# Second MLP: feature block 6 of the down projection by half-size products, block 7 over two rounds, last parts in another tile order

## The reference, cut to what matters

```python
def rms_norm(x, gain):
    y = x * lax.rsqrt(jnp.mean(x * x, axis=-1, keepdims=True) + EPS)
    return y * gain

def sq_relu_mlp(h, w_up, w_down):
    return jnp.square(jax.nn.relu(h @ w_up)) @ w_down

for i in range(DEPTH):                       # DEPTH = 2
    ...                                      # the mixer: retention, then gated DeltaNet
    ff = sq_relu_mlp(rms_norm(h, gains[2]), mlp_w_up[i], mlp_w_down[i])
    h = h + rms_norm(ff, gains[3])
```

## Time and profile before

| | us |
|---|---|
| three runs | 1400.92, 1404.13, 1404.32; median 1404.13 |
| the profiled execution | 1400.85 |
| its span, first to last instruction | 1399.1 |
| mean granted TensorE clock, share of full speed | 0.998 |
| busy: PE / DVE / ACT / POOL | 1386.6 / 948.6 / 711.4 / 289.4 |

### The profile page before, as it was taken

One profiled execution on the slowest core, in us unless ns is written; L12 is line 12 of the kernel. 1 busy time (PEld: TensorE's weight loads), 2 busy tenths in 40 slices (PEclk: granted clock), 3 DMA queues, 4 the chain that ended last, 5 costly groups with the idle time before them and its releaser, 6 DMA issues.

```text
span 1399.1 us, 19288 instructions
## 1 busy us (share of the span) xinstructions
PE 1386.6 (99%) x7537; PEld 1171.4 (84%) x7538; DVE 948.6 (68%) x1444; ACT 711.4 (51%) x1280; POOL 289.4 (21%) x159
## 2 busy tenths in 40 slices
PE   9999999999999999999999999999999999999998
PEld 7988888658899888888889988889989988888886
DVE  5869779662274877877538534797746777877735
ACT  6235455453364655455345477764835754445442
POOL 6320000443520000000151235357431000000031
PEclk9999999999999999999999999999999999999999
DMA  6522332901325323223432142221115333332131
GB/s 219 208 90 108 146 115 85 350 10 60 98 90 206 121 91 109 82 81 120 142 104 96 47 149 75 87 82 41 61 61 171 105 117 121 120 112 99 61 136 61
DMA packets 69213, 155.27 MB, mean 111 GB/s; under 512 B 4225, under 2 KB 4609, under 8 KB 67458
## 3 DMA queue, kind: packets, MB, share of 16 engines
q1 hardware_dynamic: 66514, 144.78, 30.4%
q10 hardware_dynamic: 2608, 9.25, 1.9%
HBM read 143.52 MB, written 10.50 MB: 110 GB/s over the span
## 4 chain that ended last, share of the span: by engine, by line
PE 94%; DVE 2%; ACT 2%; POOL 1%; issue 1%; DVEq 0%; ACTq 0%; POOLq 0%
PE banks L645 27%; PE banks L647 27%; PE banks L646 27%; PE banks L897 2%; PE banks L880 1%; PE banks L801 1%; PE banks L1070 1%; PE banks L1026 1%; PE banks L701 1%; POOL w_lo L525 1%; PE banks L812 1%; PE banks L915 0%; PE banks L1274 0%; PE banks L1264 0%; PE banks L787 0%
## 5 line engine op out<-in xcount | busy, mean ns | idle before, releaser
L525 POOL TENSOR_TENSOR w_lo<-w_raw,w_hi 128x1024 fp32r<-128x1024 f32 (+1 forms) x86 | 198.4, 2332 | 990.8 <-ACT w_hi L1792 602.9
L645 PE MATMUL banks<-act_hi,w_hi 128*128 128x512 f32 (+1 forms) x800 | 288.7, 361 | 0.5 <-DVE act_lo L2248 0.3
L646 PE MATMUL banks<-act_lo,w_hi 128*128 128x512 f32 (+1 forms) x800 | 287.5, 359 | 0.0
L647 PE MATMUL banks<-act_hi,w_lo 128*128 128x512 f32 (+1 forms) x800 | 287.5, 359 | 0.0
L645 PEld LDWEIGHTS banks<-act_hi,w_hi 128*128 128x128 f32 x800 | 151.1, 189 | 23.6 <-DVE act_lo L2248 0.7
L647 PEld LDWEIGHTS banks<-act_hi,w_lo 128*128 128x128 f32 x800 | 151.1, 189 | 22.6
L646 PEld LDWEIGHTS banks<-act_lo,w_hi 128*128 128x128 f32 x800 | 151.1, 189 | 22.1
L1767 ACT ACTIVATE t_hi<-quarter 128x1024 fp32r<-128x1024 f32 x84 | 88.7, 1056 | 88.1 <-PE banks L647 87.1
L645 PE MATMUL banks<-t_hi,fast_hi 128*128 128x512 f32 x336 | 130.7, 389 | 0.0
L646 PE MATMUL banks<-t_lo,fast_hi 128*128 128x512 f32 x336 | 130.7, 389 | 0.0
L647 PE MATMUL banks<-t_hi,fast_lo 128*128 128x512 f32 x336 | 130.7, 389 | 0.0
(11 more groups left out here) (343 smaller groups left out, 2930.3 us busy)
## 6 DMA issues: line engine op xcount, KB each, us to landing
w_raw<-in_mlp_w_up_dram SPq DMA_DIRECT2D x32, 1024.0 KB, 5.3
quarter<-in_mlp_w_down_dram SPq DMA_DIRECT2D x48, 512.0 KB, 6.4
w_raw<-in_gdn_w_in_dram SPq DMA_DIRECT2D x16, 1024.0 KB, 5.6
w_raw<-in_ret_w_in_dram SPq DMA_DIRECT2D x14, 1024.0 KB, 6.6
vg<-in_ret_w_in_dram SPq DMA_DIRECT2D x8, 1024.0 KB, 10.3
w_raw<-in_ret_w_out_dram SPq DMA_DIRECT2D x8, 1024.0 KB, 5.2
w_raw<-in_mlp_w_down_dram SPq DMA_DIRECT2D x8, 1024.0 KB, 5.0
kept<-resid SPq DMA_DIRECT2D x2, 2048.0 KB, 7.6
```

Of the source, the lines that this page charges most:

```text
L525: done = nc.gpsimd.tensor_tensor(LO[slot][:, kt, :], RAW[raw][:, kt, :], HI[slot][:, kt, :].bitcast(F32), ALU.subtract)
L645: pe.matmul(dst, sta_hi, mov_hi, start=first, stop=False, skip_group_check=adds)
L646: pe.matmul(dst, sta_hi, mov_lo, start=False, stop=False, skip_group_check=adds)
L647: return pe.matmul(dst, sta_lo, mov_hi, start=False, stop=last, skip_group_check=adds)
```

## The change

The second MLP has seven rounds (`FASTS = (6, 7)`); the first one is left as it was. Block 6 is computed by half-size products. The up parts of block 7 are spread over rounds 5 and 6: in round 5 the four of the first half (U0 to U3) come behind P0, P2, P4 and P6, in round 6 the four of the second half (U4 to U7) behind P0 to P3. Only block 7 goes the plain way, in eight *end parts* of 12 matmuls in the order of `END_ORDER`: halves p=0 (now in banks 4 to 7) and p=1 (banks 0 to 3) of a tile soon after each other. The down weights of block 7 are two chunks. ACT's and DVE's lists get a part of their own for round 6 and the end.

```diff
-FAST = 6
+FASTS = (6, 7)
+END_ORDER = ((0, 0), (0, 1), (1, 0), (1, 1), (0, 2), (1, 2), (0, 3), (1, 3))
...
@@ SP: stream_mlp @@
-                for u in range(FAST):
+                for u in range(6):
                     chunk(u + 3, 1)
-                    if u + 1 < FAST:
+                    if u + 1 < fast:
                         quarters(u + 1)
-                    chunk(u + 4, 0)
-                sp.wait_ge(sem("prod_full"), VG_T + 14 * FAST * (layer + 1))
+                    if u + 4 <= PARTS or fast < PARTS - 1:
+                        chunk(u + 4, 0)
+                sp.wait_ge(sem("prod_full"), VG_T + 14 * (done_before + fast))
...
@@ PE: mlp @@
+                def end_part(p, m):
+                    mm = slice(m * P, (m + 1) * P)
+                    for kt in range(CK):
+                        if m == 0:
+                            if kt % (CK // 2) == 0:
+                                pe.wait_ge(w_ready, 2 * (c1 + p) + 1 + kt // (CK // 2))
+                            pe.wait_ge(sem("hid_low"), base + 7 * fast + kt + 1)
+                        done = three(bank[4 * (1 - p) + m][:, :], plain_hi[layer][0][:, kt, mm], plain_lo[layer][0][:, kt, mm],
+                                     HI[p][:, kt, :], LO[p][:, kt, :], kt == 0, kt == CK - 1)
+                    done.then_inc(bank_full, 1)
...
+                if fast == PARTS - 1:
+                    for s in range(7):
+                        product(PARTS - 3, s)
+                        if s in (0, 2, 4, 6):
+                            up_part(PARTS - 1, s // 2)
+                    for s in range(7):
+                        product(PARTS - 2, s)
+                        if s < 4:
+                            up_part(PARTS - 1, 4 + s)
+                    pe.wait_ge(emptied, 4 * g1)
+                    for p, m in END_ORDER:
+                        if (p, m) == (1, 0):
+                            pe.wait_ge(sem("x_out"), 8 * VG + 8 * (done_before + fast))
+                            pe.wait_ge(sem("w_out"), 6 * VG + 6 * (done_before + fast))
+                        end_part(p, m)
+                    return
...
-                if layer:
-                    for m, j in ((0, 0), (1, 0), (0, 1), (1, 1), (2, 0), (2, 1), (3, 0), (3, 1)):
-                        last_part(1, m, j, m == 0)
-                    return
...
@@ ACT: mlp, round 6 @@
+                    take_tile(v, 2)
+                    plain_high(v, 0)
+                    t_high(u, 4)
+                    take_tile(v, 3)
+                    plain_high(v, 1)
+                    t_high(u, 5)
+                    plain_high(v, 2)
+                    split(PARTS, 0)
+                    t_high(u, 6)
+                    plain_high(v, 3)
+                    split(PARTS, 1)
...
@@ DVE: first_half @@
+                if b == 4:
+                    take_out(b, 0, 0, more)
+                    take_out(b, 0, 1, more)
+                    gained(0)
+                    gained(1)
+                    last_tile(0)
+                    last_tile(1)
+                    for m in (2, 3):
+                        take_out(b, 0, m, more)
+                        gained(m)
+                        last_tile(m)
+                    return
...
@@ DVE: mlp, end of round 6 @@
+                    take_product(u, 4)
+                    plain_low(v, 2)
+                    t_low(u, 6)
+                    plain_low(v, 3)
+                    take_product(u, 5)
+                    take_product(u, 6)
+                    dve.wait_ge(sem("resid_back"), 16 * (layer + 2))
+                    first_half(2 * layer + 2, True)
+                    return
```

More of the change, by code:

```diff
@@ L168, in hybrid_trunk @@
                 for b in range(2)] for a in range(2)]
-    plain_hi = [[big(f"plain_hi{a}{b}", [P, 4, T], F32R, PLAIN_AT[a][b][0]) for b in range(2)] for a in range(2)]
-    plain_lo = [[big(f"plain_lo{a}{b}", [P, 4, T], F32R, PLAIN_AT[a][b][1]) for b in range(2)] for a in range(2)]
+    plain_hi = [[big(f"plain_hi{a}{b}", [P, 4, T], F32R, at[0]) for b, at in enumerate(PLAIN_AT[a])] for a in range(2)]
+    plain_lo = [[big(f"plain_lo{a}{b}", [P, 4, T], F32R, at[1]) for b, at in enumerate(PLAIN_AT[a])] for a in range(2)]
     s3_made = big("s3_made", [P, 2, 2 * P], F32, 97)
@@ L553, in low_plain @@
                 c1 = MLP[layer][1][1]
-                for c in range(c1, c1 + 4):
+                for c in range(c1, c1 + 2 * (PARTS - FASTS[layer])):
                     pool.wait_ge(w_ready, 2 * c)
@@ L1750, in plain_high @@
                     act.wait_ge(sem("squared"), tiles + TT * v + m + 1)
-                    act.wait_ge(sem("prod_full"), VG_T + 14 * (FAST * layer + FAST - 1))
-                    act.activation(plain_hi[layer][v - FAST][:, m, :], relu[:, m, :], ACT.Copy)\
+                    act.wait_ge(sem("prod_full"), VG_T + 14 * (done_before + fast - 1))
+                    act.activation(plain_hi[layer][v - fast][:, m, :], relu[:, m, :], ACT.Copy)\
                         .then_inc(sem("hid_high"), 1)
                 def t_high(u, p):
-                    unit = FAST * layer + u
+                    unit = done_before + u
                     q = 7 * unit + p
@@ L1812, in mlp @@
                 take_tile(1, 2)
-                for u in range(FAST):
+                for u in range(fast if fast < PARTS - 1 else fast - 1):
                     w, v = u + 1, u + 2
@@ L2262, in norms @@
             def norms(b, more=False):
-                if b == 4:
-                    for m in range(TT):
-                        last_tile(m)
-                elif b:
+                if b:
                     take_out(b, 1, 0, more)
@@ L2556, in plain_low @@
                 def plain_low(v, m):
-                    dve.wait_ge(sem("hid_high"), base + 7 * FAST + 4 * (v - FAST) + m + 1)
-                    if v == PARTS - 1 and m == 0:
-                        dve.wait_ge(sem("t_ready"), VG_T + 7 * (FAST * layer + FAST - 1) + 4)
-                    dve.tensor_tensor(plain_lo[layer][v - FAST][:, m, :], relu[:, m, :],
-                                      plain_hi[layer][v - FAST][:, m, :].bitcast(F32), ALU.subtract)\
+                    dve.wait_ge(sem("hid_high"), base + 7 * fast + 4 * (v - fast) + m + 1)
+                    if layer == 0 and v == PARTS - 1 and m == 0:
+                        dve.wait_ge(sem("t_ready"), VG_T + 7 * (done_before + fast - 1) + 4)
+                    dve.tensor_tensor(plain_lo[layer][v - fast][:, m, :], relu[:, m, :],
+                                      plain_hi[layer][v - fast][:, m, :].bitcast(F32), ALU.subtract)\
                         .then_inc(sem("hid_low"), 1)
                 def add_up(u, k):
-                    unit = FAST * layer + u
+                    unit = done_before + u
                     q = 7 * unit
```

150 lines of the change are left out of this document (92 added, 58 removed).

## The result

| | before | after |
|---|---|---|
| median of the runs, us | 1404.18 (6 runs, 1400.92 to 1404.32) | 1416.59 (6 runs, 1414.23 to 1417.23) |
| the profiled execution / its span, us | 1400.85 / 1399.1 | 1417.07 / 1415.3 |
| mean granted clock | 0.998 | 0.996 |

The change makes the kernel slower: ratio 1.0092, 95% interval 1.008 to 1.0103. (A ratio compares all runs of both kernels and is not the ratio of the two medians.) The prediction said slower, 1413.5 us in a range of 1405.5 to 1418.

The account below looks back on a forecast made before the run. PE was taken to bound the kernel (busy 99% of the span). -2.72 (matmuls) + 7.8 (waits) + 5.9 (end) = +11.0 us gave 1411.9 on the profiled execution, 1415.1 on the median; middle 1413.5, range 1405.5 to 1418.

Parts of the forecast that it names:

- 12 matmuls fewer: On PE, 96 matmuls of the last parts go and 84 of seven products come: one group fewer, -2.72 us.
- P3 and P4 late: Round 5: DVE's in-order queue delivers the low parts for P3 and P4 late, 1.84 us in all.
- P5 late: Round 6: ACT's `t_hi` for P5 stands behind tile 3's relu, square and split; PE waits 1.75 us.
- P6 late: Round 6: POOL's weight split takes turns with DVE and delays the last `t_lo`; PE waits 4.2 us.
- P6 at half clock: Round 6: PE's clock falls during P6's wait, so P6 takes twice its 2.72 us; left out of the main sum.
- from the last product's end: Last product's end to span's end: late residual load, then DVE's own chain and the last store, 34.6 us.
- against 28.7 before: PE's 21.8 us of end parts plus 6.9 to the span's end; the predicted end is 5.9 us longer.
- the prediction's lower bound: Round 6, P6's wait: 0.7 us if POOL were not in the way of the last `t_lo`.
- The rival without turns: Round 6: POOL and DVE do not alternate, last wait 0.7 to 1.85 us; +7.5 to +8.7; chance 0.20.
- the clock's rival: Round 6: P6's wait lowers PE's clock and P6 takes twice its 2.72 us; +13.7, 1414.6 to 1417.8; chance 0.12.
- The end follows PE: Rounds without waits, DVE ready at each end part: saved group comes through whole, -2.7 us, 1401.4; chance 0.08.
- only the end pays: Rounds 5 and 6 absorb DVE's and ACT's lateness, the 34.6 us end remains: +3.2 us, 1407.3; chance 0.10.

Follow-up runs that it names:

- round 5's experiment: Changed kernel with one up part of round 5 (U2) moved from behind P4 to between P3 and P4: 1415.69 us, ratio 1.0103 to the kernel before.
- the last kernel: Changed kernel with rounds 5 and 6 reordered, residual loaded early, end tile by tile, half-gain and up-weight split moved later: 1400.17 us, ratio 0.9992 to the kernel before.

## Why the prediction was right, step by step

| term | predicted | measured in the profile after |
|---|---|---|
| 12 matmuls fewer | -2.72 | -2.72 (7525 matmul records for 7537) |
| P3 and P4 late | 1.84 | 1.59 (0.41 + 1.18) |
| P5 late | 1.75 | 1.57 |
| P6 late | 4.2 | 3.78 |
| P6 at half clock | 0 (a rival: +2.7) | 1.7 (4.41 - 2.72) |
| from the last product's end | 34.6 | 1415.3 - 1380.06 = 35.2 |
| against 28.7 before | +5.9 | +6.5 |
| sum | +11.0 | +12.4; whole difference +12.8 |

- **PE's waits** came where they were named, and were 0.9 less together. A part of that is the start behind a wait: it was put at 0.25 behind the end of `t_lo`, and PE started 0.09 to 0.10 behind it each time. The edits show the causes as predicted: DVE's order in round 5, ACT's order at P5, POOL's turns with DVE at P6 (and some 0.5 of ACT's order there, the 0.7 of the prediction's lower bound). The rival without turns (a last wait of 0.7 to 1.85) is out: the `t_lo` took 3.37, and without POOL beside it 1.22.
- **What was off is the clock's term.** The prediction set it to nothing and gave it 0.12 as a rival with 2.7 us. In the profile after it cost 1.7, since eight of P6's twelve matmuls ran at the lower level and not all. Filling the wait took 1.6 away.
- **The end** is as worked out: the load lands 8.3 us after its issue (7.9 predicted), DVE's tail takes 24.5 (24.3). The 0.6 on top is the load (0.4) and DVE's tail (0.2). The load's excess is scatter of the runs as far as they show: with the gains' load issued 4.7 us ahead of it in both, it took 8.29 here and 7.75 in round 5's experiment.
- **About 0.4 us** of the 12.8 stands in no term. Some 0.3 of it is seen: P3, P4 and P5, each behind a wait, take 2.83 to 2.84 us instead of 2.72. In each the second matmul starts 0.30 or 0.31 and not 0.23 behind the first.
- **How near, and by what luck.** By the medians the change costs 12.4 us; the forecast of 1413.5 is 9.4 above the median that it started from. The prediction added its sum to two bases, the profiled execution and the median 3.3 above it, and took the middle; the sum on the median, 1415.1, was the better base, and with the clock's 1.7, less 0.9 of waits, plus 0.6 at the end it comes to 1416.5. So the measured 1416.59 lies above both forms of the main sum (1411.9 and 1415.1) and in the band of the clock's rival (1414.6 to 1417.8). The waits and the end were foreseen; that the time lies inside the range is owed to the room left for that rival.
- **Rivals.** "The end follows PE" and "only the end pays" fell with PE's waits. Yet in the last kernel, after six edits, the end does follow PE. The residual early was a condition of it, as the prediction said. The half-gains ahead of the last tiles were not: there DVE still took 5.59 us per tile, and it fell behind PE's 5.44 only when the half-gain went into DVE's wait inside the last tile.

## What to carry to other kernels

A saving on the engine that sets the time shortens the rounds in which the other engines prepare its operands; lay their lists beside the new due times product by product, since an order that was free becomes a wait while the engines still have time. When a long tail of matmuls is taken away, look for what it hid: here a load of 8 us and the take-out of the last tiles, which cost more than was saved. Where a wait of several us on TensorE (PE) can't be avoided, matmuls whose result nobody reads can keep the clock up; here they took back 1.6 us, though not the wait.

## What the runs showed of the hardware

- VectorE (DVE) and GpSimd (POOL) took turns, instruction by instruction, when both worked in SBUF: beside GpSimd's tensor_tensor of 128x1024 VectorE's 1.22 us became 3.37, its 0.69 became 2.26 to 2.88. The take-out, which reads a PSUM bank too, kept its 1.21 beside the same four.
- After one and the same wait of 3.6 us the clock fell to its lower level in three profiles (matmuls 0.43 apart) and not in a fourth. With 16 matmuls in the wait it did not fall.
- At the full clock the first matmul behind a wait took 0.47 us instead of 0.39, and the second started 0.30 or 0.31 and not 0.23 behind it.
- The residual's load, 2048 KB from DRAM, landed 7.7 to 8.3 us after its issue in the five kernels that issue it with the last product's end.
